# Fourth gate unit as three rounded products, two units' remainders by adding transfers, later weights queued behind them

## What is computed

```python
h = rms_norm(x, attn_norm_g[l])
proj = jnp.matmul(h, w_in[l])            # convolution 1024, queries 512, keys 512, values 512, gates 2048
...
gates = jax.nn.sigmoid(proj[..., o3:]).reshape(B, S, N_BRANCH, D)
conv_out = conformer_conv(u_conv, ...)   # 31 taps, layer norm, silu
attn_out = diff_attention(q, k, v, lam, subln_g[l], lam_init)
merged = (gates[:, :, 0] * jnp.matmul(conv_out, w_conv_out[l])
          + gates[:, :, 1] * jnp.matmul(attn_out, w_attn_out[l]))
x = x + jnp.matmul(merged, w_out[l])
```

## Time and profile before

| | us |
|---|---|
| median of 3 runs | 1029.08 |
| lowest and highest | 1027.55, 1029.47 |
| the profiled execution | 1028.6 |
| its span, first to last instruction | 1026.8 |
| TensorE busy | 901.3 (88%) |
| VectorE busy | 459.5 (45%) |
| ScalarE busy | 366.9 (36%) |
| GpSimd busy | 8.1 (1%) |
| chain that ended last: TensorE, DMA | 63%, 28% |

### The profile page before, as it was taken

The page is one execution under the profiler, slowest core; times in us unless marked ns, Lnnn a source line. Parts: engine busy times, 40 slices in busy tenths (PEclk is TensorE's granted clock), DMA queues, the critical chain, the costliest instruction groups (busy, mean ns, idle before and its releaser), DMA issues.

```text
span 1026.8 us, 14473 instructions
## 1 busy us (share of the span) xinstructions
PE 901.3 (88%) x6088; PEld 661.2 (64%) x6088; DVE 459.5 (45%) x816; ACT 366.9 (36%) x584; POOL 8.1 (1%) x14
## 2 busy tenths in 40 slices
PE   7999999999888857768666766999999999999997
PEld 7989989864246321314122231389999999999886
DVE  6799868501010010100101010189656579888842
ACT  5565585211010000101000010248665666656631
POOL 1000000000000000000000000000100000000000
PEclk9999999999899977969887896999999999999999
DMA  9766435999999999999999999982534255654551
GB/s 326 266 228 218 152 123 221 427 390 429 414 409 429 417 431 423 425 426 427 428 422 427 421 429 424 402 289 83 159 112 162 84 163 178 207 190 165 174 195 41
DMA packets 78493, 301.27 MB, mean 293 GB/s; under 512 B 4195, under 2 KB 30948, under 8 KB 62818
## 3 DMA queue, kind: packets, MB, share of 16 engines
q1 hardware_dynamic: 76640, 298.82, 74.2%
q10 hardware_dynamic: 1458, 1.07, 0.4%
q0 software_dynamic: 336, 0.53, 0.3%
HBM read 298.84 MB, written 1.05 MB: 292 GB/s over the span
## 4 chain that ended last, share of the span: by engine, by line
PE 63%; DMA 28%; DVE 4%; ACT 3%; SPq 1%; issue 1%; DVEq 0%; PEldq 0%; ACTq 0%
PE bank L1446 11%; DMA ring<-in_w_gate_e_dram 9%; DMA ring<-in_w_down_e_dram 8%; DMA ring<-in_w_up_e_dram 8%; PE bank L1102 7%; PE bank L1464 6%; PE bank L819 3%; PE bank L789 3%; PE bank L723 3%; PE bank L1235 3%; PE bank L696 3%; PE bank L1160 3%; DMA qvpr<-in_w_down_e_dram 2%; PE bank L1326 2%; PE bank L1341 2%; PE bank L1132 2%
## 5 line engine op out<-in xcount | busy, mean ns | idle before, releaser
L1102 PE MATMUL bank<-ring,big 128*32 128x512 f32 x768 | 166.3, 714 | 79.1 <-DMA ring<-in_w_up_e_dram 41.4
L1102 PEld LDWEIGHTS bank<-ring,big 128*32 128x32 f32 x768 | 38.9, 127 | 198.7 <-issue 91.7
L354 DVE TENSOR_TENSOR ring_parts<-ring,ring_parts 128x2048 fp32r<-128x2048 f32 (+1 forms) x54 | 118.9, 2248 | 30.9 <-ACT ring_parts L346 30.6
L346 ACT ACTIVATE ring_parts<-ring 128x2048 fp32r<-128x2048 f32 (+1 forms) x53 | 96.7, 1874 | 48.3 <-DMA ring<-in_w_down_dram 22.6
L1446 PE MATMUL bank<-mrg_parts,ring_parts 128*128 128x256 f32 x640 | 82.3, 281 | 0.0
L2366 DVE TENSOR_TENSOR xT<-bank,xT 128x512 f32<-128x512 f32 x32 | 22.1, 692 | 128.7 <-PE bank L1146 128.7
L1446 PEld LDWEIGHTS bank<-mrg_parts,ring_parts 128*128 128x128 f32 x640 | 78.5, 189 | 0.0
L2323 DVE TENSOR_TENSOR big<-big,const 128x128 f32<-128x128 f32 x14 | 3.5, 289 | 155.7 <-PE bank L1089 155.7
L1102 PE MATMUL bank<-hs,big 128*32 128x512 f32 x128 | 70.4, 705 | 0.0
L1102 PE MATMUL bank<-qvpr,big 128*32 128x512 f32 x112 | 63.4, 721 | 1.1 <-DMA qvpr<-in_w_gate_e_dram 1.1
L1688 ACT ACTIVATE big<-bank 128x512 f32<-128x512 f32 x16 | 9.6, 597 | 137.6 <-PE bank L1022 137.6
(11 more groups left out here) (456 smaller groups left out, 1644.5 us busy)
## 6 DMA issues: line engine op xcount, KB each, us to landing
ring<-in_w_up_e_dram SPq DMA_DIRECT2D x24, 2048.0 KB, 29.1
ring<-in_w_gate_e_dram SPq DMA_DIRECT2D x24, 2048.0 KB, 22.1
ring<-in_w_down_e_dram SPq DMA_DIRECT2D x17, 2048.0 KB, 21.1
ring<-in_w_in_dram SPq DMA_DIRECT2D x12, 2048.0 KB, 14.4
ring<-in_w_up_dram SPq DMA_DIRECT2D x22, 1024.0 KB, 6.8
ring<-in_w_down_e_dram SPq DMA_DIRECT2D x12, 1024.0 KB, 19.9
ring<-in_w_down_dram SPq DMA_DIRECT2D x5, 2048.0 KB, 8.1
ring<-in_w_out_dram SPq DMA_DIRECT2D x4, 2048.0 KB, 9.3
```

Of the source, the lines that this page charges most:

```text
L346: signal(act.activation(pairs[stage][u % 3][0][:, part], raws[stage][u % 3][:, part], ACT.Copy), stage + "_hi")
L354: signal(eng.tensor_tensor(lo[:, part], raws[stage][u % 3][:, part], hi[:, part].bitcast(F32), ALU.subtract), name)
L1102: mm = pe.matmul(bank[part][CAP * j:CAP * j + CAP, :], xeT[:, c, CAP * j:CAP * j + CAP], w[j][c], start=(c == 0), stop=(c == DC - 1))
```

## The change

The fourth gate unit becomes rounded products too (`split_gates(3, ...)` in the places of `gates`). Its hi part goes into slot 0, where the first unit's was.

The remainders of units 2 and 3 are made in another way. ScalarE writes the negated hi part over the weights (two more activations for each unit), and GpSimd issues two transfers of 1 MB for each unit that add the weights, read once more from HBM, to it: -hi + weight. For these units the pass with the remainder is the last of the three. VectorE's remainders of unit 2 go away, and the maxima of heads 0 and 1 move from tap 15 to tap 20.

The units of `pre` get other slots (`PRE_AT`: 2, 1, 0, 3) and another order on SyncE's queue: convolution, ao, the second half of `w_out` and the early keys behind gate 11, the first half of `w_out` behind gate 15. With the slots, the order in which the experts' units 0 and 2 are loaded is exchanged. GpSimd's later transfers of the last norm's gains count on the same semaphore as the fourth unit's.

```diff
-                   [ring_r[1][:, 0:2048], ring_r[1][:, 2048:4096]]]
+                   [ring_r[1][:, 0:2048], ring_r[1][:, 2048:4096]], [ring_r[0][:, 0:2048], ring_r[0][:, 2048:4096]]]
+        PRE_AT = (2, 1, 0, 3)
+        GATE_LO_DMAS = 32
...
-            for i, last in ((0, ("gt", 3)), (2, ("gt", 3)), (3, ("gt", 7)), (1, ("gt", 11))):
-                src = pre[i]
+            for i, last in ((0, ("gt", 11)), (1, ("gt", 11)), (3, ("gt", 11)), (None, ("gt", 11)), (2, ("gt", 15))):
                 arrive(sp, last)
-                dst = ring[i % RING][:, 0:src.shape[1] * src.shape[2]].rearrange("p (k n) -> p k n", k=src.shape[1])
-                sp.dma_start(dst, src).then_inc(landed[i % RING], 16)
-            sp.dma_start(keys_w, w_xkv[:, :, 512:768]).then_inc(S["keys_early"], 16)
+                if i is None:
+                    sp.dma_start(keys_w, w_xkv[:, :, 512:768]).then_inc(S["keys_early"], 16)
+                    continue
+                src, s = pre[i], PRE_AT[i]
+                dst = ring[s][:, 0:src.shape[1] * src.shape[2]].rearrange("p (k n) -> p k n", k=src.shape[1])
+                sp.dma_start(dst, src).then_inc(landed[s], 16)
...
-                for u in (8, 2, 0, 3):
+                for u in (8, 0, 2, 3):
                     load_unit(0, u)
...
+            for u, landed_in in ((2, "gate_lo"), (3, "pool_in")):
+                for i in range(2):
+                    pool.wait_ge(S["gate_hi"], 4 * u - 4 + 2 + i + 1)
+                    dst = ring_r[PLAIN_AT[1 + u]][:, 2048 * i:2048 * i + 2048].rearrange("p (k n) -> p k n", k=4)
+                    pool.dma_start(dst, w_plain[1 + u][:, 4 * i:4 * i + 4].bitcast(F32R), accum_op=ALU.add).then_inc(S[landed_in], 16)
...
-            def split_gates(u):
+            def split_gates(u, ms=range(4)):
...
-                for m in range(4):
+                passes = ((hi, h1_hi), (lo, h1_hi), (hi, h1_lo)) if u < 2 else ((hi, h1_hi), (hi, h1_lo), (lo, h1_hi))
+                for m in ms:
                     b = begin(pe, ("gt", 4 * u + m))
...
+                                if which == 0:
+                                    pe.wait_ge(S["gate_hi"], (2 * u if u < 2 else 4 * u - 4) + k // 4 + 1)
+                                elif w is lo and u < 2:
+                                    pe.wait_ge(S["in_lo"], 10 + 2 * u + k // 4 + 1)
+                                elif w is lo and k == 0:
+                                    pe.wait_ge(S[("gate_lo", "pool_in")[u - 2]], 32)
...
-            gates(12, 1)
+            split_gates(3, (0,))
...
-            gates(13, 1)
+            split_gates(3, (1,))
...
-            gates(14, 2)
+            split_gates(3, (2, 3))
...
+                for i in range(2 if u >= 2 else 0):
+                    act.wait_ge(S["gate_hi"], 4 * u - 4 + i + 1)
+                    signal(act.activation(ring_r[PLAIN_AT[1 + u]][:, 2048 * i:2048 * i + 2048], GATE_HI[u][i].bitcast(F32), ACT.Copy,
+                                          scale=-1.0), "gate_hi")
...
             round_gates(2)
             gates(0, 4)
+            round_gates(3)
             gates(4, 4)
...
-            convolve((2, 3), ((6, keys_and_gates), (CW // 2, first_maxima)))
+            convolve((2, 3), ((6, queries_and_keys), (CW // 2 + 5, first_maxima)))
```

More of the change, by code:

```diff
@@ L365, in pre_unit @@
         def pre_unit(pe, i):
-            pe.wait_ge(landed[i % RING], 16 * (i // RING + 1))
-            return ring[i % RING]
+            pe.wait_ge(landed[PRE_AT[i]], 16)
+            return ring[PRE_AT[i]]
         def post_unit(pe, j):
@@ L660, in _ @@
                 pool.dma_start(g_row[0:1].rearrange("o (c p) -> o c p", c=DC),
-                               A["par"][:, a:b].rearrange("p c -> c p").unsqueeze(0)).then_inc(S["gain_in"], 16)
+                               A["par"][:, a:b].rearrange("p c -> c p").unsqueeze(0)).then_inc(S["pool_in"], 16)
             for i in range(7):
-                pool.wait_ge(S["gain_in"], 16 * i + 16)
-                pool.dma_start(g_row[2 ** i:2 ** (i + 1)], g_row[0:2 ** i]).then_inc(S["gain_in"], 16)
+                pool.wait_ge(S["pool_in"], GATE_LO_DMAS + 16 * i + 16)
+                pool.dma_start(g_row[2 ** i:2 ** (i + 1)], g_row[0:2 ** i]).then_inc(S["pool_in"], 16)
         @block.tensor
@@ L805, in _ @@
                 filled(mm, ("v", t))
-            def split_gates(u):
+            def split_gates(u, ms=range(4)):
                 lo = u512(ring_r[PLAIN_AT[1 + u]])
                 hi = [half.rearrange("p (k n) -> p k n", k=4) for half in GATE_HI[u]]
-                for m in range(4):
+                passes = ((hi, h1_hi), (lo, h1_hi), (hi, h1_lo)) if u < 2 else ((hi, h1_hi), (hi, h1_lo), (lo, h1_hi))
+                for m in ms:
                     b = begin(pe, ("gt", 4 * u + m))
-                    for which in range(3):
+                    for which, (w, x) in enumerate(passes):
                         for k in range(8):
[L815 to L819, removed]
+                            if m == 0 and k % 4 == 0:
+                                if which == 0:
[4 more added lines that the diff above has]
+                                    pe.wait_ge(S[("gate_lo", "pool_in")[u - 2]], 32)
+                            w_k = lo[:, k] if w is lo else hi[k // 4][:, k % 4]
+                            x_k = h1_hi[k] if x is h1_hi else h1_lo[:, k * T:k * T + T]
+                            mm = pe.matmul(b[:, 0:T], w_k[:, P * m:P * m + P], x_k, start=(which == 0 and k == 0),
                                            stop=(which == 2 and k == 7))
                     filled(mm, ("gt", 4 * u + m))
[L823 to L827, removed]
             b = begin(pe, ("qn", 0))
@@ L952, in _ @@
             for u in range(2):
-                w_lo = u512(ring_r[2 + u])
+                w_lo = u512(ring_r[PRE_AT[2 + u]])
                 if u == 1:
@@ L984, in _ @@
                         if (u, which) == (0, 1):
-                            freed.append(used[2])
+                            freed.append(used[0])
                     if u == 1 and ms[0] < 3:
@@ L988, in _ @@
                 if u == 0:
-                    freed.append(used[0])
+                    freed.append(used[2])
             route((6, 7))
@@ L1640, in round_out @@
             def round_out(u, i):
-                act.wait_ge(landed[2 + u], 16)
+                act.wait_ge(landed[PRE_AT[2 + u]], 16)
                 a, b, part = OUT_HI[u][i]
@@ L1646, in round_out @@
                         copied(act, ("co", m))
-                signal(act.activation(part, ring[2 + u][:, 512 * a:512 * b], ACT.Copy), "out_hi")
+                signal(act.activation(part, ring[PRE_AT[2 + u]][:, 512 * a:512 * b], ACT.Copy), "out_hi")
             arrive(act, ("co", 7))
@@ L2172, in rest_of_out @@
                 at = slice(512 * a, 512 * b)
-                signal(dve.tensor_tensor(ring_r[2 + u][:, at], ring[2 + u][:, at], part.bitcast(F32), ALU.subtract), "out_lo")
+                s = PRE_AT[2 + u]
+                signal(dve.tensor_tensor(ring_r[s][:, at], ring[s][:, at], part.bitcast(F32), ALU.subtract), "out_lo")
             rest_of_out(0, 0)
@@ L2609, in _ @@
                 rest_of_both("ff", u)
-            dve.wait_ge(S["gain_in"], 128)
+            dve.wait_ge(S["pool_in"], GATE_LO_DMAS + 128)
             for t in range(TT):
```

10 lines of the change are left out of this document (4 added, 6 removed).

## The result

The changed kernel took **1032.59 us** in the median of 7 runs (1031.1 to 1034.6), the kernel before 1028.64 on the same chip (7 runs, 1027.01 to 1029.49). The ratio is 1.0041, 95% interval 1.0029 to 1.0052: 3.95 us slower. The forecast was 1030.2; the range of 1027.0 to 1033.0 held the median, but "within 0.2%", which had the chance 0.70, did not come, and "slower", which had 0.24, did. That the range held is luck: its upper part stood there for late adding transfers (rival B), and those were in time.

A forecast was written before the change was run, and what follows sets the result against it. TensorE alone bounds 99 to 138 us, DMA the expert stage from 164. Gates -2.25, co's wait +2.7, fourth head +0.7 give about +1.1 us at o1: profiled 1028.6 becomes 1029.7, median 1030.2, range 1027.0 to 1033.0.

The forecast's parts named there:

- rival B: Gates 8 and 12, third pass: adding transfers come late, 1031.3 us at a third of the plain rate, 1041.7 at a quarter; chance 0.20.
- Gates, -2.25 us: TensorE, gates 12 to 15: 11.56 us as rounded products in place of 13.81, so co could start at 128.03.
- ScalarE's six activations at no cost: ScalarE, 80 to 107 us: six added halves of 1.85 us, 11.1 us in all, covered by 13.8 us idle.
- Adding transfers in time: GpSimd's queue before gates 8 and 12: four added 1 MB transfers land before TensorE asks for them, at no cost.
- the point of decision: Gates 8 and 12: adding rate below which late transfers make the kernel slower, 15.5 us a pair, 136 GB/s.
- Ao lands late: SyncE's queue behind gate 11: ao lands at 123.7, ScalarE stands 3.5 us, TensorE waits 2.7 us before co.
- The bound of 124.5: Latest landing of ao allowed for in place of 123.7, moving the sum to +1.9 us at o1.
- Nothing for the clock: TensorE at co: no term for a lower clock after its wait; co starts after 130.7 and is done at 137.6.
- Fourth turned head, +0.7 us: Behind co: VectorE's last differences end at 138.5, so TensorE waits for the fourth head and starts o1 at 138.9.
- Nothing late next, expert stage passes the shift on: From o1 on: last output half lands near 137, ahead of o1; expert stage from 164 us moves by as much.
- rival C: Expert stage: already queued loads fill the gap and the change of start is lost, 1029.1 us; chance 0.08.
- Rival A: In front of co: the wait for ao does not show, o1 comes 2.1 us sooner, 1027.0 us; chance 0.10.

The follow-up runs named there:

- Experiment 1: Changed kernel with ao's load issued first and the convolution's weights second behind gate 11: 1025.96 us, ratio 0.9975 to the kernel before.
- experiment 6: Changed kernel with the convolution's weights loaded behind gate 3 and one half of the output weights behind gate 7, as before the change: 1034.67 us, ratio 1.0061.
- seventh experiment: Changed kernel repeated twice, 1030.83 and 1033.26 us; ao-first kernel repeated, 1025.78; changed kernel with five dummy matmuls before the router's last narrow ones, 1033.02.
- Experiment 2: Changed kernel with seven more identity matmuls on TensorE in front of its wait for conv_out, ao still late: 1030.88 us, ratio 1.0024.
- experiment 3: Kernel before the change, with only the five loads in the changed order and behind the changed gates: 1029.04 us, ratio 1.0007.
- experiment 5: Changed kernel with the convolution's weights issued behind gate 7 in place of gate 11: 1027.31 us, ratio 0.9985 to the kernel before.
- experiment 4: Changed kernel with ao third behind gate 11, after the convolution's weights and the second output half: 1038.82 us, ratio 1.0096.

## Why the prediction was right and wrong, step by step

- **Gates, -2.25 us: held.** Without the wait co would have started at 125.78, 28.78 us behind gate 8 in place of 31.25, 2.47 us sooner; the 0.2 us over are in the pieces around the gates. Experiment 1 has the same 28.79.
- **ScalarE's six activations at no cost: held.** ScalarE is busy longer between 86 and 107 us (15.91 us; the earlier trace rows has 9.62), and TensorE has no idle time in gate 8 or in any gate behind it.
- **Adding transfers in time: held, but not by the value taken.** I took the upper half of 210 to 395 GB/s as the likelier. They moved at 207, just under the lower end, which came from a row of this very queue. The chip's plain loads in the expert stage moved at 418 to 434 (windows above). The Trainium skill (Collectives: The Full Stack, section "The bandwidth ceiling: the fold count and why AG ≠ RS ≠ AR") states for a collective that its add needs two source reads and so runs at about half the rate of a copy. The ratio in this trace agrees with it, 207 against 418; that the second read is the reason no run here shows. The choice cost nothing in the sum, since the point of decision was at 136. B did not come; experiment 6 brought it about by putting loads beside the transfers.
- **Ao lands late: the mechanism held, its size was too small.** I had 12.7 us for a 2 MB load behind another, from the one longest of four loads, and added 0.4 for the issue. Measured: 13.93 (13.9 again in both repeats in the seventh experiment, 13.7 in the second). With it the arrival of 123.7 - 99.03 = 24.7 us behind gate 8 became 122.93 - 97.00 = 25.9. ScalarE waited 4.84 us in place of 3.5, TensorE 4.15 in place of 2.7. Hence co started 1.68 us late in place of 0.4. The bound of 124.5, 25.5 us behind gate 8, was also too near. What it left out: I treated the queue as one load after the other. From 109.00 to 122.93 the DMA engines moved 366 GB/s, that is 5.1 MB; the two loads are 4.2 MB. So about 0.9 MB of what was queued behind ao landed before ao's last packet. In experiment 3 the same sum gives 365 GB/s x 12.32 us = 4.5 MB, 0.3 MB over. Why the share differs is open, and so is whether it is the whole reason for the longer load; that the loads behind take a part is in both.
- **Nothing for the clock: the step that was missing.** The prediction gave co its old 6.91 us. A wait of TensorE was costed at its own length, but 4.15 us of idle time were followed by the clock of 0.50, and co took 1.92 us more. Experiment 2 took the idle time away and left the late load: co was 1.66 us shorter. The other 0.2 to 0.3 us are not the clock's: co takes 7.1 us at 1.00 in experiments 1 and 5 too. At 1.7 us the clock's term is still larger than the error of any other.
- **Fourth turned head, +0.7 us: did not show.** VectorE's last differences were late, but co ended later still. Experiment 2 uncovers the wait, at 0.16 us. The path itself is real: in experiment 3 the chain that ended last runs through the exponentials, VectorE's differences and the fourth turned head to o1, 0.68 us late.
- **Nothing late next, expert stage passes the shift on: held** (3.6 us at 165.65, rival C out), but a second, smaller fall of the clock added 0.97 us.
- **Rival A: right as a mechanism.** It had ao's wait not show and o1 2.1 us sooner; experiment 1 made that happen with one swap, -2.26 us at o1 and -1.8 us in the medians. The prediction didn't ask whether the order of the two loads was needed.

The forecast of +1.1 us at o1 and the measured +3.61 thus differ by +1.3 (co's start: the wait 1.45 us longer, the gates 0.2 better), +1.9 (co's length), and -0.7 (the head). The second fall adds about 1.

## What to carry to other kernels

When loads are queued behind one event, put them in the order in which their users first wait, counting the whole chain behind the load: ao was used by TensorE after co's weights, but ScalarE's preparation of it stood in front of the product that co needed. When a step on the busiest engine gets shorter, look for the load that it now arrives ahead of: the saving becomes idle time, and on TensorE it can be paid again as a low clock in the work behind it (here 1.7 us in co after 4.15 us of waiting). Where an edit needs the DMA engines to itself, as the adding transfers did here, sort anew what is pushed back: the same edit lost 0.4% with ao second in the queue and gained 0.25% with ao first.

## What the runs showed of the hardware

- Adding transfers from DRAM into SBUF moved 207 GB/s with the DMA engines full (share 1.13), half of the 418 to 434 of the plain loads in the expert stage. In the same profile an issue took 1.26 to 1.48 us on GpSimd, and 1 MB landed after 9.6 to 13.3 us.
- A plain 2 MB load beside them made the last add 5.6 us later, and took 15.7 us itself instead of 7.8 (experiment 5).
- A load of 2 MB behind another on SyncE's queue landed 12.3 to 14.0 us after its issue, ao behind two others after 18.9 (experiment 4); the loads queued behind it take a part of the engines' time before it is done.
- After 4.1 us without work TensorE's clock was granted at 0.50 in the first part of co, which took 8.60 to 9.36 us in the profiles of the changed kernel. After 9.65 us without work co took 10.17 (experiment 4). After waits of 1.42 us (experiment 5), 1.15 us (experiment 6) and under 0.1 us (experiment 3) the clock stayed at 1.00.
- The clock also fell to 0.50 behind a stretch of narrow matmuls with only 0.61 us of idle time, in 6 of the 11 profiles that have the same sequence there, and not in the one with dummy matmuls ahead of it.
